# When the routing's scattered DMAs, two lookups and a small turn are done, in a mixer and mixture-of-experts kernel on one Trainium2 core

## The reference, cut to what matters

```python
def moe_ffn(h, ...):
    logits = xt @ w_router + b_router
    top_vals, top_idx = lax.top_k(logits, 4)
    top_gates = jax.nn.softmax(top_vals, axis=-1)
    ...                                    # rows sorted by expert, blocks of 128
    gate = jnp.minimum(xb @ w_gate[e] + b_gate[e], 7.0)
    up = jnp.clip(xb @ w_up[e] + b_up[e], -7.0, 7.0)
    glu = gate * jax.nn.sigmoid(1.702 * gate)
    y = (glu * (up + 1.0)) @ w_down[e] + b_down[e]
    out = segment_sum(y * gate_of_the_row, token_of_the_row)

x = x + hybrid_mixer(rmsnorm(x)); x = x + moe_ffn(rmsnorm(x)); x = second_block(x)
```

## Time and profile before

| | |
|---|---|
| median of three runs | 1695.19 us |
| profiled execution | 1695.1 us |
| its span | 1693.8 us |
| PE, DVE, ACT, POOL busy | 1618.2, 1345.5, 1197.5, 238.0 us |
| chain that ended last, by engine | PE 76%, DVE 13%, ACT 7%, issue 4%, DMA 0% |
| DMA, mean | 286 GB/s, 483.66 MB |

### The profile page before, as it was taken

One profiled execution on the slowest core, in us unless ns is written; L12 is line 12 of the kernel. 1 busy time (PEld: TensorE's weight loads), 2 busy tenths in 40 slices (PEclk: granted clock), 3 DMA queues, 4 the chain that ended last, 5 costly groups with the idle time before them and its releaser, 6 DMA issues.

```text
span 1693.8 us, 19448 instructions
## 1 busy us (share of the span) xinstructions
PE 1618.2 (96%) x7479; PEld 1309.3 (77%) x7479; DVE 1345.5 (79%) x1041; ACT 1197.5 (71%) x932; POOL 238.0 (14%) x170
## 2 busy tenths in 40 slices
PE   6999988999999999999999999999998999999998
PEld 5877877877877877877877877877866877778886
DVE  4476689999999999999999999999987235764343
ACT  4354358888888888888888888888875356763232
POOL 1502027131120120120120120120020000000000
PEclk9999979999999999999999999999999999999999
DMA  8411379999999999999999999999993312113211
GB/s 291 134 51 75 123 267 330 402 405 415 414 407 416 414 408 416 410 408 412 408 410 408 412 410 410 409 410 401 393 351 111 125 50 75 50 57 125 96 66 50
DMA packets 96191, 483.66 MB, mean 286 GB/s; under 512 B 14517, under 2 KB 16237, under 8 KB 46944
## 3 DMA queue, kind: packets, MB, share of 16 engines
q1 hardware_dynamic: 81696, 459.50, 68.1%
q0 software_dynamic: 10480, 18.17, 4.2%
q10 hardware_dynamic: 3920, 4.72, 0.8%
HBM read 475.91 MB, written 22.99 MB: 295 GB/s over the span
## 4 chain that ended last, share of the span: by engine, by line
PE 76%; DVE 13%; ACT 7%; issue 4%; DMA 0%; SPq 0%; DVEq 0%; ACTq 0%
PE PS L561 67%; ACT WH L1076 5%; DVE low L1428 4%; DVE WL L1428 4%; PE PS L803 4%; PE PS L1011 2%; DVE eu L1774 1%; DVE eu L1779 1%; PE PS L1023 1%; PE PS L817 1%; PE PS L593 1%; DVE hl L1765 1%; PE PS L673 0%; PE PS L1004 0%; DMA ring<-in_w_in_dram 0%
## 5 line engine op out<-in xcount | busy, mean ns | idle before, releaser
L1076 ACT ACTIVATE WH<-land 128x2048 fp32r<-128x2048 f32 x210 | 396.6, 1912 | 132.6 <-PE PS L561 131.8
L1076 ACT ACTIVATE WH<-ring 128x2048 fp32r<-128x2048 f32 x218 | 411.7, 1912 | 90.9 <-PE PS L561 86.5
L1428 DVE TENSOR_TENSOR low<-ring,WH 128x2048 fp32r<-128x2048 f32 x194 | 437.0, 2286 | 19.7 <-ACT WH L1076 18.8
L1428 DVE TENSOR_TENSOR WL<-land,WH 128x2048 fp32r<-128x2048 f32 x190 | 427.3, 2285 | 20.4 <-ACT WH L1076 19.8
L561 PE MATMUL PS<-WH,xh 128*128 128x512 f32 x512 | 161.0, 396 | 4.1 <-DVE low L1428 1.9
L2119 POOL DMA_INDIRECT accd<-ys,lists x28 | 60.1, 2146 | 742.9 <-ACT ys L1266 734.2
L561 PE MATMUL PS<-WH,hh 128*128 128x512 f32 x512 | 148.4, 391 | 0.0
L561 PE MATMUL PS<-WH,xs 128*128 128x512 f32 x512 | 145.1, 407 | 1.8 <-DVE xs L1763 1.8
L561 PE MATMUL PS<-WH,xl 128*128 128x512 f32 x512 | 137.3, 390 | 0.0
L1428 DVE TENSOR_TENSOR WL<-ring,WH 128x2048 fp32r<-128x2048 f32 x24 | 54.8, 2288 | 82.5 <-ACT WH L1076 82.5
L561 PEld LDWEIGHTS PS<-WH,xs 128*128 128x128 f32 x512 | 98.5, 195 | 22.0 <-issue 2.2
(11 more groups left out here) (434 smaller groups left out, 2961.6 us busy)
## 6 DMA issues: line engine op xcount, KB each, us to landing
land<-in_w_up_dram SPq DMA_DIRECT2D x71, 1024.0 KB, 9.3
ring<-in_w_down_dram SPq DMA_DIRECT2D x71, 1024.0 KB, 10.1
ring<-in_w_gate_dram SPq DMA_DIRECT2D x66, 1024.0 KB, 9.8
land<-in_w_gate_dram SPq DMA_DIRECT2D x62, 1024.0 KB, 10.5
ring<-in_w_up_dram SPq DMA_DIRECT2D x57, 1024.0 KB, 9.8
land<-in_w_down_dram SPq DMA_DIRECT2D x57, 1024.0 KB, 10.0
ring<-in_w_in_dram SPq DMA_DIRECT2D x19, 1024.0 KB, 5.8
land<-in_w_in_dram SPq DMA_DIRECT2D x13, 1024.0 KB, 5.3
```

Of the source, the lines that this page charges most:

```text
L1076: A.activation(WH[buf[n]], lands[spot[n]], ACT.Copy).then_inc(s_hi, 1)
L1428: V.tensor_tensor(WLn[n], lands[spot[n]], WH[buf[n]].bitcast(F32), SUB).then_inc(s_lo, 1)
```

## The change

It moves work, and removes and adds none.

- SP issues the four DMAs that begin the sums after the loads of expert 0's weights, and only once the gather of expert 0's rows has landed (and all of X is there), all four in a row. Before, the first three stood ahead of the load of g5, and the fourth behind that of g7.
- DVE does `vector_slots`, the further count and the spreading of Gt earlier, and the two lookups of experts 1 and 2 later.
- POOL writes the first 2 of the 16 list DMAs ahead of the gathers of experts 1 and 2, and the other 14 behind them.
- The four transposes of Gt and the copy to GtT move from expert 0 to expert 1. They use bank 6 in place of bank 5, so that they wait until DVE has read the turned middle result of expert 0. PE waits for the copy before it turns the rows of expert 2, no longer before expert 0's first down product.

The core of the diff:

```diff
@@ sync_experts
-            if p == 5:
-                for j in range(3):
-                    sums_begin(j)
             load(n_g[0, p])
-        sums_begin(3)
+        S.wait_ge(s_xg[0], 16)
+        S.wait_ge(s_x1, 8)
+        for j in range(4):
+            S.dma_start(accv[j], X[:, j]).then_inc(s_acc, 16)
@@ tensor_turn_rows
+        if e == 2:
+            P.wait_ge(s_spk, 1)
         tensor_turn8(xg[e % 2])
@@ tensor_gate_up
             tensor_turn_rows(1)
-            P.wait_ge(s_ix, NI)
+        if p == 5 and e == 1:
+            P.wait_ge(s_tl, t_mid[0] + 1)
             P.wait_ge(s_sp, 1)
             for j in range(4):
-                last = P.transpose(PS[0:32, 5, ...], Gt[:, j], ident)
+                last = P.transpose(PS[0:32, 6, ...], Gt[:, j], ident)
             last.then_inc(s_spt, 1)
@@ tensor_down
-            if e == 0:
-                P.wait_ge(s_spk, 1)
@@ scalar_experts
                     scalar_gate(e)
+                if (what, p) == ("g", 6) and e == 1:
+                    A.wait_ge(s_spt, 1)
+                    A.activation(GtT, PS[0:32, 6, :]...).then_inc(s_spk, 1)
                 if (what, p) == ("g", 7) and e == 0:
                     scalar_rows(1)
-                    A.wait_ge(s_spt, 1)
-                    A.activation(GtT, PS[0:32, 5, :]...).then_inc(s_spk, 1)
@@ vector_experts
+        vector_slots()
         low(first + 3)
-        vector_index(1, 4)
-        vector_slots()
-        vector_index(2, 5)
+        vector_further_count()
+        spread_out(Gt, GK).then_inc(s_sp, 1)
         low(first + NX - 1)
-        spread_out(Gt, GK).then_inc(s_sp, 1)
-        vector_further_count()
...
                 low(ahead(...))
+                if e == 0 and p + 1 < NI:
+                    vector_index(p + 1, 4 + p)
@@ gpsimd_experts
+        G.wait_ge(s_sig, 3)
+        G.wait_ge(s_small, 144)
+        gpsimd_list(0, 2)
         gpsimd_gather(1)
         gpsimd_gather(2)
-        G.wait_ge(s_sig, 3)
-        G.wait_ge(s_small, 144)
-        gpsimd_list(0, 16)
+        gpsimd_list(2, 16)
```

More of the change, by code:

```diff
@@ L497, in rows_of @@
         return w[0, bass.ds(ex, 1), 256 * kc:256 * kc + 256].rearrange("a (p k) f -> p (a k f)", k=2)
-    def sums_begin(j):
-        S.wait_ge(s_x1, 2 * j + 2)
-        S.dma_start(accv[j], X[:, j]).then_inc(s_acc, 16)
     def sync_experts():
         for p in range(8):
-            if p == 5:
-                for j in range(3):
-                    sums_begin(j)
             load(n_g[0, p])
-        sums_begin(3)
+        S.wait_ge(s_xg[0], 16)
+        S.wait_ge(s_x1, 8)
+        for j in range(4):
+            S.dma_start(accv[j], X[:, j]).then_inc(s_acc, 16)
         S.wait_ge(s_sig, 1)
@@ L894, in tensor_gate_up @@
             tensor_turn_rows(1)
-            P.wait_ge(s_ix, NI)
+        if p == 5 and e == 1:
+            P.wait_ge(s_tl, t_mid[0] + 1)
             P.wait_ge(s_sp, 1)
             for j in range(4):
-                last = P.transpose(PS[0:32, 5, 128 * j:128 * j + 128], Gt[:, j], ident)
+                last = P.transpose(PS[0:32, 6, 128 * j:128 * j + 128], Gt[:, j], ident)
             last.then_inc(s_spt, 1)
@@ L1291, in scalar_experts @@
                     scalar_gate(e)
+                if (what, p) == ("g", 6) and e == 1:
+                    A.wait_ge(s_spt, 1)
+                    A.activation(GtT, PS[0:32, 6, :].rearrange("p (j t) -> p j t", j=4), ACT.Copy).then_inc(s_spk, 1)
                 if (what, p) == ("g", 7) and e == 0:
                     scalar_rows(1)
-                    A.wait_ge(s_spt, 1)
-                    A.activation(GtT, PS[0:32, 5, :].rearrange("p (j t) -> p j t", j=4), ACT.Copy).then_inc(s_spk, 1)
         A.activation(st[:, 28:29], C[:, EPS5:EPS5 + 1], ACT.Sqrt)
```

## The result

The changed kernel takes 1703.57 us (median of six runs, 1703.02 to 1708.95), the kernel before 1695.14 us (six runs, 1693.35 to 1697.29): ratio 1.0055, interval 1.0044 to 1.0067. It is slower by 8.4 us, within the range, 0.9 us under the forecast. Its profiled execution took 1704.04 us, its span is 1702.7 us. PE is busy for 1616.8 us (before 1618.2), although the span is 8.9 us longer: on balance what was added is idle time. (Work at the slower clock counts as busy, and both executions have some; where it lies is read from the stages.)

What follows compares the result with a forecast made beforehand. PE was taken to bound the kernel, so what delays it for good delays the end. Gt's 6.7 us plus 2.7 of clock, the other four terms 0, gave 9.4 us on 1695.1: 1704.5 us, range 1699.5 to 1708.0.

Steps and rivals of the forecast that it cites:

- The turn of Gt: Expert 1: PE pauses 2.99 us before Gt's transposes and 4.4 before the turn of expert 2's rows, 6.7 us later.
- That it reaches the end: Loop of PE, ACT and DVE through the later experts: the 6.7 us carries to the end, nothing gives it back.
- rivals 2 and 3: DMA engines bind and hide PE's pauses, 1697.3 us, 6%; later start frees the loop's wait for eu, 1680.1 us, 4%.
- The clock: Behind expert 1's two new PE pauses: clock falls to half speed, 1.5 us plus 1.2 us, together 2.7 us.
- The gathers: Expert 1's rows, wanted by PE near 261.4 us: later gather lands in time; 0 to 1.0 us, taken as 0.
- Rival 1: Gather of expert 1's rows lands late, delaying PE's turn, xs and the chain; another clock fall; 1707.0 us, 13%.
- The sums: Four DMAs, 2.10 MB, ahead of expert 1's loads: stream behind by 2.2 us, hidden by PE's delay; taken as 0.
- DVE's order to 256 us: DVE up to g6's low part: same work reordered, PE waits about 2 us for g3's low part; cost 0.
- The lists: 14 list DMAs behind the gathers: 2 us later, hidden before ACT's output of expert 0; cost 0.

Runs made afterwards that it cites:

- e3: Kernel before with only the move of Gt's transposes and copy, ACT's copy to GtT ahead of the high part and gate: 1699.3 us, ratio 1.0022.
- e10: Kernel before with the Gt move alone, plus unused products on PE in both pauses (six and nine): 1701.57 us, ratio 1.0039.
- e1: Kernel before with only the move of Gt's transposes and the copy to GtT; sums, DVE's and POOL's order stay: 1703.94 us, ratio 1.0048.
- e4: Kernel before with the Gt move alone, plus nine unused products on PE in the second pause only: 1703.22 us, ratio 1.0043.
- e2: Changed kernel with Gt's transposes and copy put back to expert 0; sums, DVE's and POOL's order new: 1696.45 us, ratio 1.0009 to before.
- e7: Kernel before with DVE multiplying the gate into eu one low part earlier in every expert, at g1: 1705.8 us, ratio 1.0067.
- e5: Kernel before with DVE's and POOL's new order alone; sums and Gt stay: 1694.97 us, ratio 0.9996.
- e6: Kernel before with the sums' four DMAs moved alone: 1694.02 us, ratio 0.9995.

## Why the prediction held, point by point

- **The turn of Gt, 6.7 us: right in size and place.** From the restart behind hl to the turn of expert 2's rows it is 8.18 us (291.93 - 283.75), before 1.53 (285.52 - 283.99): 6.65 us more. Forecast pauses 2.99 and 4.4, measured 2.84 and 4.36; the copy first on ACT took the second away (e3). With the clock held, the loss in that piece is 6.70 us (e10).
- **That it reaches the end: right.** From 348.70 to 1246.03 us the changed kernel takes 897.33 us for 14 pairs of experts, before 897.70. Nothing is caught up, and rivals 2 and 3 are out.
- **The clock, 2.7 us: near in size, wrong in its working.** Measured 64.95 - 56.21 - 6.70 = 2.04 us, and 3.2 in e1. I took 1.5 us for one fall from the stage at 468.5 us, and that is the price where nothing behind it waits. At 468 us itself it is not paid: the next restart of that kind comes 64.17 us later, and where no fall follows 63.95 us, since the 1.03 us of waiting for hl soaks it up. Behind the new pauses there is no such wait until 348 us. I had it surely behind the longer one and in four of five behind the shorter; it fell behind the longer each time it was left open (2 of 2: after, e1), behind the shorter in three of four (e1, e3, e4, not after). And the term is not the whole of the clock: in the changed kernel there was the fall behind the gather besides (next point).
- **The gathers, 0 to 1.0 us, taken as 0: mis-sized.** The step that failed is "I take 0", with its reason "the measured pair is from there". The two gathers of the earlier trace rows ran while the queues had room; with the sums' four DMAs in them the same gather took 9.93 us, and from then on the path was 1.9 to 2.3 us longer (51.28 and 51.73 against 49.4). The lateness alone was nearly covered: counted from the rows of expert 0, PE's turn starts at 29.13 us (261.60 - 232.47), before at 26.78, so 2.35 us late where the prediction allowed 1.77 + 0.35 = 2.12. What that cover left out is the clock, which fell behind the 2.68 us of waiting: an estimated 1.6 us (5.39 - 3.8), and with it most of the 1.9. No run fills that pause, so this split is not shown. Rival 1 had the late landing and priced a fall of the clock at 1.5 us, but put the fall behind the pause at 284 us and the way to the end through xs; it went through PE's place in WH, ACT's high part and DVE's 1.90 us of waiting for it.
- **The sums, 0: mis-sized too**, by the pieces and in the other direction: they had cost the routing 1.0 us by standing in the way of h2d's stores, which no view of before showed, because in that execution DVE came later than the stores.
- **DVE's order to 256 us, 0: right.** g6's low part starts at 253.40 us, 20.93 us behind the rows of expert 0 at 232.47; before it was 255.64 - 234.62 = 21.02. PE waited 0.64 us for g3, not 2, and 1.15 us for g4.
- **The lists, 0: right.** ACT does not wait for them at 308.85 us.
- **The sum.** Gt 6.7, clock 2.0, gathers 1.9, routing -1.0: 9.6 us by the pieces (the profiled execution's luck in the routing left out), and 8.4 by the medians; Gt alone is 8.3 (e1), the rest 0.8 (e2). The interval of the medians, 1.0044 to 1.0067, is 7.5 to 11.4 us and holds both. The forecast of 9.4 was near in part by luck: two terms set to 0 came out at 1.9 and -1.0 us, of opposite sign.

What stays open: why the clock keeps at some pauses and not at others of the same length (e7's alternate), and what sets the two lengths of the routing. All four executions with the sums moved had the short one, of the nine others five; that the move favours the short one is not excluded, and would widen the medians' gain in the routing beyond 1.0 us.

## What to carry to other kernels

Before a wait is added to a full engine, list what stands ahead of its releaser in that engine's own order: a copy of 0.57 us cost 4.4 us, because three instructions that hung on the waiting engine stood before it. A pause on the path costs its length and, in most cases here, the slower clock behind it, unless a wait follows that soaks this up. That holds for a wait that seems covered too: count the clock behind it before calling it covered. A transfer's latency is read from the stretch with the traffic that the change will leave there, not from the one that it had.

## What the runs showed of the hardware

- The granted clock fell (to 0.50 in the changed kernel's 292 to 296 us) behind many of PE's pauses of 2.2 to 4.4 us, with PE busy before them, and cost 1.5 to 2.0 us each where no wait followed. Behind e1's 2.23 us of waiting for xs it fell too (0.61 from 267.6 to 272 us) and cost some 0.3 us, since a wait for eu followed (49.66 against 49.40 and 49.43 in e4 and e10, where it stayed). The Trainium skill, "TensorE: Matmul & The Clock Gate", section "HAM oscillation — how this bites in real kernels", tells of a matmul kernel that pays for the clock again at each wait for a load, where it could have paid once; the trace agrees, but not at every pause (e7: seven of fourteen pauses of 2.51 us).
- Unused matmuls in the two pauses held it at 1.00 (e10), at no cost to the path.
- One 512 KB gather by an indirect DMA took 5.5 us with the DMA engines at 0.90, 7.9 us 9 us later in the stream (e5, 0.85), and 8.6 to 11.0 us with four more DMAs of 512 KB in the queues (e6, 1.02; after, 0.99; e2, 0.98).
- PE's stop of 4.36 us emptied the weight stream: 0.04 of the DMA engines in the 4 us behind it, and yet nothing waited for a load later.
